# Expert blocks ranked by load: halves of two experts in one block, results sent out by row, three blocks in four turned by VectorE

## What is computed

```python
def _moe(x, router_w, router_bias, w_gate, w_up, w_down, sh_gate, sh_up, sh_down):
    scores = jax.nn.sigmoid((t @ router_w).astype(jnp.float32))
    _, idx = lax.top_k(scores + router_bias.astype(jnp.float32), TOP_K)
    sel = jnp.take_along_axis(scores, idx, axis=-1)
    wts = sel / jnp.sum(sel, axis=-1, keepdims=True) * ROUTED_SCALE
    gates = jnp.einsum('tk,tke->te', wts, jax.nn.one_hot(idx, N_EXPERTS, dtype=jnp.float32)).astype(x.dtype)
    hid = jax.nn.silu(jnp.einsum('td,edf->tef', t, w_gate)) * jnp.einsum('td,edf->tef', t, w_up)
    routed = jnp.einsum('tef,efd->td', hid * gates[..., None], w_down)
    shared = (jax.nn.silu(t @ sh_gate) * (t @ sh_up)) @ sh_down
    return (routed + shared).reshape(bsz, l, d)
```

## Time and profile before

| | |
|---|---|
| runs, us | 1449.41, 1452.12, 1452.35 (median 1452.12) |
| span of the profiled execution, us | 1449.8; its time outside the span is not listed apart |
| PE, DVE, ACT, POOL busy | 92%, 47%, 28%, 21% |
| DMA moved | 286.36 MB, mean 198 GB/s |
| HBM read and written | 237.52 MB and 64.56 MB |

### The profile page before, as it was taken

One profiled execution on the slowest core, in us unless ns is written; L12 is line 12 of the kernel. 1 busy time (PEld: TensorE's weight loads), 2 busy tenths in 40 slices (PEclk: granted clock), 3 DMA queues, 4 the chain that ended last, 5 costly groups with the idle time before them and its releaser, 6 DMA issues. The chain is left out here.

```text
span 1449.8 us, 21596 instructions
## 1 busy us (share of the span) xinstructions
PE 1337.0 (92%) x8160; PEld 996.5 (69%) x8160; DVE 685.5 (47%) x1254; ACT 412.0 (28%) x796; POOL 301.5 (21%) x440
## 2 busy tenths in 40 slices
PE   5999999999899998999799999999999999999664
PEld 1678666777899986555545457688888888887521
DVE  2698738202665663777576226432222222222156
ACT  3212221215556554233131025321222122212111
POOL 0200100102321311454440210211111111111173
PEclk9999999999999999999899999999999999999998
DMA  9656667121433341000120401799999999998696
GB/s 360 209 174 186 201 43 59 58 73 30 182 153 100 127 175 34 8 5 31 37 103 23 175 0 44 281 385 393 384 378 384 378 397 382 398 385 307 212 382 264
DMA packets 111005, 286.36 MB, mean 198 GB/s; under 512 B 28677, under 2 KB 46639, under 8 KB 109528
## 3 DMA queue, kind: packets, MB, share of 16 engines
q1 hardware_dynamic: 95096, 242.15, 48.6%
q0 software_dynamic: 15840, 43.28, 7.8%
HBM read 237.52 MB, written 64.56 MB: 208 GB/s over the span
## 5 line engine op out<-in xcount | busy, mean ns | idle before, releaser
L2771 PEld LDWEIGHTS PS<-arena 128*128 128x128 f32 x2240 | 258.5, 192 | 43.3 <-ACT arena L3310 26.2
L2771 PE MATMUL PS<-arena 128*128 128x128 f32 x2240 | 263.1, 276 | 5.2 <-DMA arena<-in_exp_w_down 3.9
L3098 DVE TENSOR_SCALAR arena<-PS,arena 128x1024 f32<-128x1024 f32 x70 | 89.9, 1284 | 141.6 <-PE PS L2779 141.6
L2779 PE MATMUL PS<-arena 128*128 128x512 f32 x280 | 137.8, 615 | 0.8 <-DVE arena L3091 0.8
L895 PE MATMUL PS<-arena 128*128 128x320 f32 x384 | 109.4, 438 | 1.5 <-DVE arena L1317 1.5
L3316 ACT ACTIVATE arena<-PS 128x128 f32<-128x128 f32 x70 | 19.4, 277 | 312.7 <-issue 176.7
L900 PE MATMUL PS<-arena 128*128 128x320 f32 x384 | 107.3, 432 | 0.0
L3091 DVE TENSOR_TENSOR arena<-arena,PS 128x128 f32<-128x128 f32 x70 | 20.1, 288 | 182.8 <-ACT arena L3316 93.4
L895 PEld LDWEIGHTS PS<-arena 128*128 128x128 f32 x384 | 73.0, 192 | 33.3 <-issue 2.9
L900 PEld LDWEIGHTS PS<-arena 128*128 128x128 f32 x384 | 73.0, 190 | 30.4
L3403 POOL DMA_INDIRECT arena<-h_rows,arena x70 | 72.1, 1030 | 58.4 <-POOL arena L3400 57.6
(11 more groups left out here) (478 smaller groups left out, 2078.0 us busy)
## 6 DMA issues: line engine op xcount, KB each, us to landing
arena<-in_exp_w_gate SPq DMA_DIRECT2D x70, 512.0 KB
arena<-in_exp_w_up SPq DMA_DIRECT2D x70, 512.0 KB
arena<-in_exp_w_down SPq DMA_DIRECT2D x70, 512.0 KB
y_rows<-arena SPq DMA_DIRECT2D x70, 512.0 KB
arena<-in_w_in SPq DMA_DIRECT2D x16, 1024.0 KB, 6.2
arena<-in_w_mod SPq DMA_DIRECT2D x32, 512.0 KB, 3.7
y_rows<-cst SPq DMA_DIRECT2D x2, 5632.0 KB, 18.5
y_rows<-cst SPq DMA_DIRECT2D x2, 5120.0 KB, 18.0
```

The lines of the kernel that those rows point to most:

```text
L2771: mm = pe.matmul(PS[:, bank, 0:P], w[:, k, :], xT[j % 2][:, k, :], start=k == 0, stop=k == KT - 1)
L2779: mm = pe.matmul(PS[:, 4 + 2 * (j % 2) + half, :], hid[j % 2], ed[j][:, 512 * half:512 * half + 512], start=True, stop=True)
L3098: dve.tensor_scalar(yb[j].rearrange("p (h n) -> p h n", h=2), PS[:, 4 + 2 * (j % 2):6 + 2 * (j % 2), :], gate_col[j % 2], None, ALU.mult). ...
```

## The change

**Ranks.** DVE makes one key for each expert from its count (its number breaks ties), and PE counts how many keys lie above it. That is the expert's rank. Two matmuls turn constants by rank into rows by expert: where its slots start, how many it has, and where the rest go.

**Capacities.** Ranks 0 to 45 have a whole block. Ranks 0 to 7 may use another half block (64 slots), ranks 48 to 63 have only half a block, and what is left over goes to the counted loop. A paired block holds two halves: for ranks 0 to 7 the rest of rank r and all of rank 56+r, for the others two ranks from 48 to 55. Ranks 46 and 47 are always the first two blocks of the counted loop, which runs one turn more than the spill needs. The 58 fixed blocks are written out in a list, without a loop: whole r, then its paired block, for r from 0 to 7; then the others, with four paired blocks among them.

```diff
-COLS = NE + SPILL + 2
-ROW_W = D + NE
+WIDE, MIDDLE = 8, 48
+WHOLE = MIDDLE - 2
+SHARED = WIDE + (NE - MIDDLE - WIDE) // 2
+STATIC = WHOLE + SHARED
+COLS = STATIC + 2 + SPILL + NE - MIDDLE + 2
...
+        for r in range(WIDE):
+            whole(r)
+            loads.append(NE - WIDE + r)
+            blocks.append((WHOLE + r, (len(loads) - 2, len(loads) - 1)))
+        for r in range(WIDE, WHOLE):
+            whole(r)
+            if r % 8 == 6 and r < 8 * (SHARED - WIDE) + WIDE:
+                n = r // 8 - 1
+                loads += [MIDDLE + 2 * n, MIDDLE + 2 * n + 1]
+                blocks.append((WHOLE + WIDE + n, (len(loads) - 2, len(loads) - 1)))
```

**Loads.** SP reads the expert of each rank from `block_expert` and loads when the last block that used the slot is done. In the counted loop it waits for the stored results instead:

```diff
+                def load_rank(n):
+                    e = sp.value_load(block_expert[0:1, loads[n]:loads[n] + 1], min_val=0, max_val=NE - 1)
+                    if n >= U:
+                        sp.wait_ge(e_ps, last_use[n - U] + 1)
+                    load_block(e, n % U)
...
+                with sp.Fori(0, groups) as i:
                     for j in range(2):
-                        spill_load(2 * i + j, j, 2 * i + (NE - 1 + j))
-                        store_block(2 * i + (NE - 2 + j), j)
-                for j in range(2):
-                    store_block(2 * groups + (NE - 2 + j), j)
+                        e = sp.value_load(block_expert[0:1, bass.ds(2 * i + (NE + j), 1)], min_val=0, max_val=NE - 1)
+                        sp.wait_ge(e_out[LIST + j], 16 * i + 16 * (STATIC // U))
+                        load_block(e, LIST + j)
```

**Paired block.** The tokens of each half are the stationary operand (64 columns) and the weights stream through; each half writes its own half of the PSUM partitions. The hidden values come out with tokens on the partitions, so one more transpose turns them (`turn_halves`):

```diff
+                def gate_up_halves(p, used):
+                    for k in range(KT):
+                        for n, j in enumerate(used):
+                            r = slice(HD * n, HD * n + HD)
+                            both = ew[j][:, 0:2 * D].rearrange("p (w k f) -> p k w f", w=2, k=KT)[:, k]
+                            mm = pe.matmul(PS[r, p, 0:2 * P].rearrange("p (w f) -> p w f", w=2), xT[p][:, k, r], both,
+                                           start=k == 0, stop=k == KT - 1)
+                    mm.then_inc(e_gu, 1)
```

```diff
+                def turn_x(b):
+
+                    j = b % U
+                    dve.wait_ge(e_x[j], fetched(b))
+                    if b >= 2:
+                        dve.wait_ge(e_gu, b - 1)
+                    dve.transpose(xT[j % 2].rearrange("p k (g s) -> p g k s", s=32),
+                                  xg[j].rearrange("p g (i k) -> p g k i", i=32)).then_inc(e_turn, 1)
```

```diff
+                LAG = 5
+                for b in range(STATIC):
+                    fetch(b)
+                    if b >= LAG:
+                        store(b - LAG)
+                for b in range(STATIC - LAG, STATIC - 2):
+                    store(b)
```

More of the change, by code:

```diff
@@ L2775, in down, with turn_halves @@
+                def turn_halves(b):
+                    pe.wait_ge(e_mid, halves[b])
+                    pe.transpose(PS[:, b % 2, 2 * P:3 * P], mid[b % 2], ident).then_inc(e_mT, 1)
+                def down(b, p, used, first=False):
                     pe.wait_ge(e_hid, b + 1)
@@ new lines, in _ @@
+                down(STATIC - 1, (STATIC - 1) % 2, [n % U for n in blocks[-1][1]])
+                groups = group_count(pe)
+                with pe.Fori(0, groups) as i:
+                    for j in range(2):
+                        transpose_x(None, LIST + j, 16 * i + (ROUNDS_X[j] + 16))
+                        if j:
+                            down(2 * i + STATIC, 0, [LIST])
+                        pe.wait_ge(e_w[LIST + j], 48 * i + 48 * (len(loads) // U + 1))
+                        pe.wait_ge(e_xT, 2 * i + (COPIES + j + 1))
+                        gate_up(j, LIST + j)
+                    down(2 * i + (STATIC + 1), 1, [LIST + 1])
@@ L3101, in own, with gates_of @@
+                def gates_of(t):
+                    if t:
+                        dve.wait_ge(g_of, t)
+                    dve_order.done(dve.tensor_tensor(chosen, spread(D1[:, t, :], 1, TOPK), spread(d8[:, t, :], 2, NE), ALU.is_equal))
+                    dve_order.done(dve.tensor_tensor(chosen, chosen, spread(gate[:, t, :], 1, TOPK), ALU.mult))
+                    dve.tensor_reduce(gate_of[:, t, :], chosen, AX.X, ALU.add).then_inc(g_of, 1)
                 def own(t):
@@ new lines, in turned_middle @@
+                def turned_middle(b):
+                    dve.wait_ge(e_mT, halves[b])
+                    if b >= 2:
+                        dve.wait_ge(e_ps, b - 1)
+                    dve.tensor_copy(hid[b % 2], PS[:, b % 2, 2 * P:3 * P]).then_inc(e_hid, 1)
+                turn_x(1)
+                for b, (_, used) in enumerate(blocks):
+                    if len(used) > 1:
+                        middle(b)
+                    else:
+                        hidden(b, b % U, b < 2)
+                    if b + 2 < STATIC and by_vector(b + 2) is not None:
+                        turn_x(b + 2)
+                    if len(used) > 1:
+                        turned_middle(b)
+                    if b < NT:
+                        own(b)
+                    elif b < 2 * NT:
+                        gates_of(b - NT)
```

535 lines of the change are left out of this document (321 added, 214 removed).

## The result

The changed kernel takes 1460.17 us (median of 5 runs, 1456.26 to 1463.49). The kernel before took 1450.03 beside it (1449.07 to 1452.35). The ratio is 1.0065, with a 95% interval of 1.0047 to 1.0083: slower by 0.65%, where 1407 and a gain of 3% had been forecast.

A forecast was written before the change was run, and what follows sets the result against it. The prediction took PE and DMA to be level bounds in the blocks; -57.8 + 10.1 + 6.6 - 4.1 = -45.2 gave a span of 1404.6 us and a median near 1407, range 1383 to 1440.

The forecast's parts named there:

- Number of blocks, loads, bytes: Expert blocks: 60 blocks in place of 70, 64 weight loads in place of 70, 142.6 MB moved.
- Before the blocks, +10.1: Ranking and tables ahead of the first block: 10.1 us later, bounds 5 and 16.
- Block 1, +6.6: Second block: PE waits 4.3 us for quarter-row tokens and 2.3 more for VectorE's turn; bounds 2 and 12.
- Halves side by side: Paired blocks: both column halves run together on PE, about 5.7 us a block; one after the other 10.9.
- VectorE's turn, 1.28 us: Token turning on VectorE in 43 blocks: 1.28 us each, bounds 0.64 to 2.56, late only above 3.6.
- GpSimd, 17 requests at 1.33 us: Indirect DMAs per four blocks: 22.6 us of issuing against 25.8 for the blocks, so covered.
- the rival that it becomes the bound: Blocks: slower GpSimd requests set the pace, up to 1.88 us each and 1496 us total; chance 0.11.
- First 16 blocks, 104 us: Alternating heavy and paired blocks: eight cycles of 13 us, set by weight loads released two at a time.
- it does less than it says: First cycles: paired blocks hold weights so long that load latency sets 16 us a cycle, 1431 total; chance 0.10.
- Other blocks, 270 us: 38 whole and 4 paired blocks: DMA binds at 266 us against PE's 237, plus 4 to the last down matmul.
- The loop, 15: Counted loop after the fixed blocks: two blocks take 15 us, waiting for results and a weight load.
- After the blocks, -4.1: Gathering of results, now issued by SyncE: 4.1 us less, bounds -6 and +5.

The follow-up runs named there:

- after_rows: Changed kernel with every block's tokens fetched by one request of whole rows, VectorE's turn kept (so the numbers computed differ): 1463.26 us, ratio 1.0086.
- split_release: Changed kernel with gate and up loads asked for once their set's gate/up matmuls are done, the down load after its down matmuls: 1429.06 us, ratio 0.9847.
- down_first: Changed kernel with TensorE running the previous block's down matmuls ahead of a block's gate/up, as in the kernel before: 1438.15 us, ratio 0.9928.
- down_first_quick: down_first with VectorE copying a paired block's turned hidden product before turning the tokens of block b+2: 1424.13 us, ratio 0.9827.
- down_first_tensor: down_first with all blocks fetched by whole rows and turned by TensorE, none by VectorE: 1424.54 us, ratio 0.9804.
- tensor_five: down_first_tensor with a fifth weight set: 1415.85 us, ratio 0.9758.
- quick_five: down_first_quick with a fifth weight set: 1415.82 us, ratio 0.9747.
- mixed_order: split_release with TensorE running the previous block's down matmuls ahead of gate/up, except behind a paired block: 1494.14 us, ratio 1.0297.

## Why the prediction was wrong

By its own steps, with the end of each stretch as the timeline of the changed kernel has it:

- *Number of blocks, loads, bytes*: right. 60 blocks, 64 loads. 307 GB/s over 456.57 us are 140 MB, for 142.6.
- *Before the blocks, +10.1*: first gate matmul at 930.29, not 933; +7.4, in its bounds. (Its parts, 3.5, 4 and 2, make 9.5, where the prediction goes on with 10.5.)
- *Block 1, +6.6*: the wait for the turn was 6.3 us.
- *Halves side by side*: right, shown with 128 contraction rows: 32 steps of 256 columns in 3.62 us. The Trainium skill ("TensorEngine Tiling (Array Packing)", Key Properties) says that tiles run independently; the trace agrees.
- *VectorE's turn, 1.28 us*: 2.03, inside 0.64 to 2.56. It was said to be late only above 3.6 us, and PE waited for it once. What it delays on VectorE's queue wasn't looked at; in the order down first that was worth 14 us.
- *GpSimd, 17 requests at 1.33 us*: right (1.02 and 0.30 between), and the rival that it becomes the bound was wrong: after_rows.
- *First 16 blocks, 104 us*: with the 6.6 of block 1 110.6 were forecast, and 123.4 passed (to 1053.7). A cycle was 15.0 us in the mean of the last seven, not 13. The rival "it does less than it says" had this cycle at 16 us and gave it one chance in ten. It named the right kind of cause, weights held too long, but in the first cycles alone, and ended at 1431.
- ***Other blocks, 270 us*: the step that failed.** "PE needs 42 times 5.65, 237, so DMA binds": this takes for granted that the queue of loads stays full. The blocks took 312.6 us (1053.7 to 1366.3). DMA was full when it had work: 399 GB/s in 1101 to 1108, a little above the 387 of the earlier trace rows. The Trainium skill ("DMA: Bandwidth & Descriptors", Specifications) has about 358 GB/s of HBM for a core, as half of what two cores share. Here one core runs alone, so 387 and 399 don't disagree with it, as the prediction had it. But DMA was busy only 89% of the time. The edit behind it stood in the change, and was costed nowhere: the place of the down matmuls on TensorE, which sets when a set is given back. Four runs show that this is the cause. With the earlier release of split_release the kernel takes 31 us less, and with the old order of down_first 22 less (36 with the swap of down_first_quick). The kernel before, with later loads, takes 10 to 84 more. In down_first the 42 blocks take 275.2 us from down to down, so the DMA time of 270 was nearly right once the loads were asked for in time.
- *The loop, 15*: 20.6 us.
- *After the blocks, -4.1*: 71.0 us from the last down matmul, for 80.3 in the earlier trace rows; -9.3, outside its bounds of -6 and +5. No run asks why.

930.3 + 123.4 + 312.6 + 20.6 + 71.0 is 1457.9, the span. Of the 53 us above the sum of 1404.6, 43 are the one step. (The prediction's -57.8 should be -57.6, and halfway between 1372 and 1407 is 1389, not 1385; neither matters.) Part of that is the clock, which falls where PE waits. The groups of gate/up steps in the changed kernel (count, busy us, mean ns of one):

```profile
L2872 PE MATMUL PS<-arena 128*128 128x128 f32 x1536 | 195.6, 289 | 45.3 <-DMA arena<-in_exp_w_down 42.9 <-ACT arena L3472 2.4
...
L2880 PE MATMUL PS<-arena 128*64 128x256 f32 x384 | 55.6, 454 | 37.0 <-issue 30.6 <-DVE arena L3236 6.3
```

and, of whole blocks in down_first_quick and of paired ones in down_first:

```profile
L2872 PE MATMUL PS<-arena 128*128 128x128 f32 x1536 | 180.7, 276 | 2.4 <-ACT arena L3472 2.4
```

```profile
L2880 PE MATMUL PS<-arena 128*64 128x256 f32 x384 | 44.9, 387 | 4.8 <-issue 4.8
```

In busy time that is 15 and 11 us more, on top of 82 of waiting ahead of these steps.

The saving in TensorE work (0.88 us a block) was worth 6 us in the new order, which holds each set 4.6 us longer. Where the old order stays, the transposes stand in a gap that is there anyway, and turning by VectorE gives nothing (down_first_tensor and down_first_quick, 1424.5 and 1424.1; tensor_five and quick_five, 1415.8 each). The prediction had no term for this gap either. In down_first_quick PE still waits 32.1 us for the hidden product, and 1424 stays 17 us above the forecast of 1407.

## What to carry to other kernels

When two resources stand level, ask for each buffer how long it is held and what is left of the ring for the transfer: buffers times block time, less the holding time, against issue to landing in a full queue. An edit that swaps two stages on the consumer changes the holding time even if it adds no work. And before moving work off an engine, look at whether it fills a gap that a dependency leaves there.

## What the runs showed of the hardware

- A core's 16 DMA engines moved 399 GB/s in 7 us (weights and tokens in, results out) at a share of 1.03.
- PE's granted clock was 0.83 in the mean of 1101 to 1108, in which PE idled, 0.50 in 1108 to 1110, and 0.92 over all blocks, against 1.00 before.
- Two halves of 64 columns at 128 contraction rows cost what one whole block does: 3.62 us for 32 steps of 256 columns, beside 3.57 for 32 of 128 x 128.
- VectorE's turn of 128 x 1024 words took 2.03 us, TensorE's eight transposes of as much 0.88.
- With quarter fetches, five sets and gate/up first, PE and SyncE issued instructions 0.7 to 2.1 us apart for up to 10 us at a time, beginning at the higher clock level. There and in mixed_order, with four sets, ScalarE's step behind gate/up started up to 11.9 and 6.3 us after their end, for 0.04 us as a rule. The cause is open.
